# Attention by groups: scores, masks and maxima of the wide tiles one branch at a time, and ScalarE without waits for its own copies and exponentials

## The reference, cut to what matters

```
p_c = masked_softmax(q k_cmp^T * scale)      # 31 compressed blocks
o_s = masked_softmax(q ks^T * scale) vs      # selected blocks; 8 blocks of 64, top 16: all of them, so plain causal
o_w = masked_softmax(q kw^T * scale) vw      # window of 512 of 512 tokens: plain causal too
o   = o_c*gate0 + o_s*gate1 + o_w*gate2
```

## Time and profile before

| | us |
|---|---|
| median of 3 runs | 1486.77 (1486.64 to 1486.95) |
| the profiled execution, time | 1486.48 |
| its span, first to last instruction | 1484.7 |
| PE busy in the span | 1458.0 (98%) |
| DVE busy | 719.7 (48%) |
| ACT busy | 711.5 (48%) |
| POOL busy | 687.1 (46%) |

### The profile page before, as it was taken

The page is one execution under the profiler, slowest core; times in us unless marked ns, Lnnn a source line. Parts: engine busy times, 40 slices in busy tenths (PEclk is TensorE's granted clock), DMA queues, the critical chain, the costliest instruction groups (busy, mean ns, idle before and its releaser), DMA issues.

```text
span 1484.7 us, 23343 instructions
## 1 busy us (share of the span) xinstructions
PE 1458.0 (98%) x7494; PEld 1205.4 (81%) x7494; DVE 719.7 (48%) x1258; ACT 711.5 (48%) x1295; POOL 687.1 (46%) x982
## 2 busy tenths in 40 slices
PE   8999999999999999999999999999999999999998
PEld 6877777888888888888888788888888888888887
DVE  6477774644434300345486767673643444400053
ACT  5245556644444423456464646464654444423262
POOL 5544446665655655364321111203465655655452
PEclk9999999999999999999999999999999999999999
DMA  6311113333222223142410100101233222233221
GB/s 231 105 66 57 57 43 114 128 99 99 86 103 94 99 100 99 57 173 81 143 58 15 44 29 28 40 17 43 100 104 103 90 99 99 95 103 100 85 99 57
DMA packets 38139, 127.80 MB, mean 86 GB/s; under 512 B 6208, under 2 KB 6976, under 8 KB 37824
## 3 DMA queue, kind: packets, MB, share of 16 engines
q1 hardware_dynamic: 32832, 117.46, 23.6%
q10 hardware_dynamic: 5248, 9.55, 1.9%
HBM read 124.90 MB, written 2.10 MB: 86 GB/s over the span
## 4 chain that ended last, share of the span: by engine, by line
PE 41%; issue 33%; POOL 21%; DVE 2%; ACT 2%; DMA 1%; POOLq 0%; SPq 0%; DVEq 0%; ACTq 0%
POOL w_lo L317 21%; PE banks_a L1299 21%; PE banks_a L1309 8%; PE banks_b L1309 7%; PE banks_b L1486 2%; PE banks_a L1505 1%; PE banks_a L1272 1%; DMA x<-in_x 1%; ACT y L384 0%; DVE xn L845 0%; PE banks_b L1489 0%; PE banks_b L1272 0%; ACT w_hi L381 0%; ACT pT L638 0%; DVE amix L1032 0%
## 5 line engine op out<-in xcount | busy, mean ns | idle before, releaser
L317 POOL TENSOR_TENSOR w_lo<-w_raw,w_hi 128x256 fp32r<-128x256 f32 x864 | 657.8, 793 | 737.0 <-ACT w_hi L381 736.7
L381 ACT ACTIVATE w_hi<-w_raw 128x1024 fp32r<-128x1024 f32 x216 | 228.5, 1061 | 271.9 <-PE banks_b L1309 116.2
L1299 PE MATMUL banks_a<-nT_hi,w_hi 128*128 128x512 f32 (+1 forms) x968 | 343.7, 376 | 0.0
L1299 PE MATMUL banks_a<-nT_lo,w_hi 128*128 128x512 f32 (+1 forms) x968 | 342.6, 375 | 0.7 <-DVE nT_lo L851 0.7
L1299 PE MATMUL banks_a<-nT_hi,w_lo 128*128 128x512 f32 (+1 forms) x968 | 341.3, 374 | 0.1
L1299 PEld LDWEIGHTS banks_a<-nT_hi,w_lo 128*128 128x128 f32 x968 | 173.3, 188 | 32.5 <-POOL w_lo L317 0.3
L1299 PEld LDWEIGHTS banks_a<-nT_lo,w_hi 128*128 128x128 f32 x968 | 173.4, 188 | 31.7 <-DVE nT_lo L851 0.9
L1299 PEld LDWEIGHTS banks_a<-nT_hi,w_hi 128*128 128x128 f32 x968 | 173.3, 188 | 31.8 <-ACT nT_hi L414 0.3
L923 DVE SCALAR_TENSOR_TENSOR y<-banks_a,conv,y 128x511 f32<-128x511 f32 x88 | 66.0, 750 | 217.7 <-ACT y L507 217.2
L507 ACT ACTIVATE y<-banks_a,conv 128x512 f32<-128x512 f32 x88 | 68.6, 779 | 206.7 <-PE banks_a L1299 206.6
L1020 DVE TENSOR_REDUCE nm<-banks_b 128x2 f32<-128x256 f32 (+2 forms) x96 | 79.2, 824 | 22.1 <-PE banks_b L1489 10.1
(11 more groups left out here) (275 smaller groups left out, 2364.8 us busy)
## 6 DMA issues: line engine op xcount, KB each, us to landing
w_raw<-in_w SPq DMA_DIRECT2D x216, 512.0 KB, 3.2
g_pre<-in_gains ACTq DMA_DIRECT2D x6, 512.0 KB, 4.9
x<-in_x SPq DMA_DIRECT2D x4, 512.0 KB, 8.5
g_post<-in_gains ACTq DMA_DIRECT2D x4, 512.0 KB, 5.3
out<-x SPq DMA_DIRECT2D x8, 256.0 KB, 2.0
pe_raw<-in_pT ACTq DMA_DIRECT2D x2, 512.0 KB, 5.2
w1k<-in_w ACTq DMA_DIRECT2D x1, 1024.0 KB, 7.0
w1v<-in_w ACTq DMA_DIRECT2D x1, 1024.0 KB, 7.4
```

The source lines that it names most:

```text
L317: pool.tensor_tensor(w_lo[slot][:, cols], w_raw[k % RAW][:, cols], w_hi[slot][:, cols].bitcast(F32), ALU.subtract).then_inc(S["w_lo_done"], 1)
L381: act.activation(w_hi[u % RING][:, :], w_raw[u % RAW][:, :], ACT.Copy).then_inc(S["w_hi_done"], 1)
L1299: m = pe.matmul(bank[:, cols], w[:, k * P:(k + 1) * P], r[:, k, cols], start=(k, pas) == (0, 0), stop=(k, pas) == (KT - 1, 2))
```

## The change

Three edits, all inside the groups.

1. PE: for a wide tile the mask of branch 0 stands right behind its two score matmuls, ahead of branch 1's. Semaphore `gscores_done` rises by 1 with each, as before.
2. DVE: `gmaxima` reduces a wide tile in two instructions, one for each branch, each as soon as its branch is scored. Narrow tiles keep the one reduce. `gnegmax_done` now counts two for each tile, and the own wait of DVE behind it is gone. The helper `maxima`, still used by differential attention, loses an argument.
3. ACT: the exponential of branch c waits for the maximum of branch c only. The exponentials and the copies of `gpT`, `vT`, `pcT` and `Vg` no longer wait for themselves.

```
 # act, gexps
-                        act.wait_ge(S["gnegmax_done"], step(h, k) + 1)
+                        act.wait_ge(S["gnegmax_done"], 2 * step(h, k) + c + 1)
...
-                        signal(act.activation(gp[:, k % 2, c, 0:n], score_columns(k)[:, c, :], ACT.Exp,
-                                              bias=nm[:, qt, c:c + 1],
-                                              accum_out=sums[:, h % 2, qt, c:c + 1]),
-                               "gprobs_done", 2 * step(h, k) + c + 1)
+                        act.activation(gp[:, k % 2, c, 0:n], score_columns(k)[:, c, :], ACT.Exp,
+                                       bias=nm[:, qt, c:c + 1],
+                                       accum_out=sums[:, h % 2, qt, c:c + 1]).then_inc(S["gprobs_done"], 1)
 # act, gp_turned; vT, pcT and Vg in the same way
-                    signal(act.activation(gpT[:, k % 2, 0, 0:n], A[2][:, 0:n], ACT.Copy), "gpTa_done",
-                           step(h, k) + 1)
+                    act.activation(gpT[:, k % 2, 0, 0:n], A[2][:, 0:n], ACT.Copy).then_inc(S["gpTa_done"], 1)
 # dve, gmaxima
-                    maxima(ORDER[k], 2 * (k % 2), "gscores_done", "gnegmax_done", step(h, k), score_columns(k))
+                    qt, both = ORDER[k], score_columns(k)
+                    if qt < 2:
+                        dve.wait_ge(S["gscores_done"], 2 * step(h, k) + 2)
+                        dve.tensor_reduce(nm[:, qt, :], both, AX.X, ALU.max, negate=True)\
+                            .then_inc(S["gnegmax_done"], 2)
+                        return
+                    for c in range(2):
+                        dve.wait_ge(S["gscores_done"], 2 * step(h, k) + c + 1)
+                        dve.tensor_reduce(nm[:, qt, c:c + 1], both[:, c, :], AX.X, ALU.max, negate=True)\
+                            .then_inc(S["gnegmax_done"], 1)
 # pe, gscores, wide tiles
                     for c in range(2):
 
                         for K in (Kh, Kl):
                             pe.matmul(both[:, c, :], Q[h][:, tok(qt)], K[:, c, 0:n], start=K is Kh, stop=False)
-                    for c in range(2):
                         pe.matmul(both[:, c, n - P:n], ident_b[:, :], causal_b[:, :], start=False,
                                   stop=True).then_inc(S["gscores_done"], 1)
```

More of the change, by code:

```diff
@@ L794, in group @@
                 act.wait_ge(S["units_done"], PLAN["group"] + 4 * g + 4)
-                signal(act.activation(vT[:, :], A[2], ACT.Copy), "vT_done", g + 1)
+                act.activation(vT[:, :], A[2], ACT.Copy).then_inc(S["vT_done"], 1)
                 gexps(*seq[0])
                 act.wait_ge(S["cpT_done"], g + 1)
-                signal(act.activation(pcT[:, :, :], A[1].rearrange("p (t n) -> p t n", t=TT), ACT.Copy),
-                       "cpTc_done", g + 1)
+                act.activation(pcT[:, :, :], A[1].rearrange("p (t n) -> p t n", t=TT), ACT.Copy)\
+                    .then_inc(S["cpTc_done"], 1)
                 act.wait_ge(S["vTt_done"], g + 1)
                 v3 = A[0].rearrange("p (t n) -> p t n", t=TT)
-                signal(act.activation(Vg[:, :, :], v3, ACT.Copy), "vg_done", g + 1)
+                act.activation(Vg[:, :, :], v3, ACT.Copy).then_inc(S["vg_done"], 1)
                 gexps(*seq[1])
@@ L1011, in _, with maxima @@
                            4 * half + t + 1)
-            def maxima(qt, b, scores, negmax, step, columns=None):
+            def maxima(qt, b, scores, negmax, step):
                 n = (qt + 1) * P
                 dve.wait_ge(S[scores], 2 * step + 2)
-                if columns is None:
-                    columns = banks_b[:, b:b + 2, 0:n]
-                signal(dve.tensor_reduce(nm[:, qt, :], columns, AX.X, ALU.max, negate=True), negmax, step + 1)
+                signal(dve.tensor_reduce(nm[:, qt, :], banks_b[:, b:b + 2, 0:n], AX.X, ALU.max, negate=True), negmax, step + 1)
             def mix(h, p, qt):
```

## The result

| | before | after |
|---|---|---|
| median of 5 runs each, us | 1486.77 (1485.63 to 1486.95) | 1474.31 (1473.92 to 1475.85) |
| ratio | | 0.9919, 95% interval 0.9904 to 0.9933 |
| profiled execution, time and span | 1486.48, 1484.7 | 1473.99, 1472.2 |

The kernel is faster by 12.5 us, 0.8%.

A forecast was written before the change was run, and what follows sets the result against it. PE was taken as the bound, stalled twice a head by the chain through reduce, exponentials and copy. Saving 2.00 us in each of four groups, 8.0 us, gave 1478.5 profiled, 1478.8 median, range 1475.3 to 1482.8.

The forecast's parts named there:

- What bounds the kernel: Middle heads: a chain through ACT stalls PE 0.55 us at k=1, 0.25 at k=3; without stalls 9.59 us a head.
- The mask's break: PE, wide tiles: a matmul behind the early mask comes 0.08 us later; bounds 0 and 0.28, 32 wide tiles.
- Two reduces: DVE, 512-wide tile: two reduces take 1.41 us against 1.23 for one, 0.18 more, hidden while DVE waits for PE.
- ScalarE's own waits: ACT's exponentials and copies without waiting for themselves: at most 0.12 us for each of three instructions, booked as nothing.
- The first head: First head of a group: DVE's longer reduce makes the k=2 transposes 0.1 us later; PE's idleness becomes a wait there.
- The last head: Last head of a group: k=3 transposes wait 0.61 us by the no-stall rule; DVE's later copy allows 0.35 back.
- The sum: Each group: stalls of 1.65, 0.50 and 0.35 gained, less 0.40 and 0.10, gives 2.00 us; four groups 8.0 us.
- The rival "more": ACT's saved 0.1 us an instruction carries the first head, up to 0.7 more a group: 11 us, 1475.8; chance 12%.

## Why the prediction was half right

- *What bounds the kernel:* right. Two stalls a head, ended by the chain through maxima and exponentials; both are gone and PE is the bound at 9.56 us where I had 9.59 (9.68 in the first of the two middle heads).
- *The mask's break, 0.08 us:* right, 0.08 in the kernel with it alone.
- *Two reduces:* the size was off, 1.29 against my 1.41 (0.06 more than one reduce, not 0.18), since I took the gap from the pair at L1156, and two reduces without a wait between them overlap by 0.09. It changed little: in the middle heads DVE has room. The Trainium skill's rule of large tiles, in "Advanced Engine Details and Errata", section The Read-Write Bubble, speaks against the split; here the split costs DVE 0.06 us a tile.
- *ScalarE's own waits, "I take nothing from it":* the step that failed. I gave 0.12 us for each instruction as the most and booked nothing. Measured it is 0.14 (0.81 to 0.67 for 512 columns), and 0.28 (0.95 to 0.67) once each exponential also waits for its own branch, a cost of the split that I had not seen. It is not slack at the ends of a group: 0.61 us for the third (68.01 and 67.40), and 2.3 us between the first milestone and the end of the span, by the difference of the two kernels.
- *The first head:* I had it 0.1 us worse; it is 0.31 better to the k = 2 transposes (6.68 against 6.99), and 0.21 worse with the own waits kept. The mechanism (DVE decides, the stall moves to k = 2) came true only without the own waits; with them ScalarE still holds k = 1, by 0.85 us.
- *The last head:* I allowed 0.35 of the 0.61 back because DVE's copy seemed to be 0.18 later. All of it came: the k = 3 transposes of the third group start 2.17 behind those of k = 2 (925.99 to 928.16). With the own waits kept 0.33 came, near my number, but by luck: ScalarE held the transposes there and not DVE, with reduces of the same size. It is the own waits once more.
- *The sum:* 2.00 us a group forecast, 2.06 measured in the third group of the kernel with own waits (1.99 to 2.62 over the four), 2.66 to 2.96 with all edits. That 2.06 is so near 2.00 is in part luck, since that kernel's exponentials are dearer than my working had them. The rival "more" named this mechanism at 12% and 11 us; it was the case that came.
- *The whole miss:* I said 1478.5 for the profiled execution and it took 1473.99. Of these 4.5 us the own waits are 2.3, the rest of the groups 0.8 (8.8 with own waits kept, not 8.0, most of it in the first group), and 1.4 lie ahead of the groups and are not the change's. Without that last part the time would have been inside the range.
- *The base:* my range took the median before as it stood, 1486.77. In the two later sets of rounds it is 1.2 us lower, and the difference to the kernel after is 11.5 us instead of 12.5.

## What to carry to other kernels

An instruction that waits for itself cost ScalarE 0.13 to 0.14 us each time here, 0.28 with a second wait behind it, and in a chain that another engine waits for that is time of the kernel: price such waits before anything is split or moved, since here they bring nearly as much alone (1.87 us a group) as the reordering does (2.06), for less text. Two edits on one chain don't add: work out where the next bound lies (here PE's own pace) and cap the sum there. And measure by a period inside the kernel where two versions differ by less than their starts.

## What the runs showed of the hardware that I had not expected

An engine's tiny instruction can wait for POOL. In the kernel after `weights_of_branches` begins like this, DVE first, POOL in the second fence:

```profile
902.49 0.73 DVE L1152 TENSOR_SCALAR st<-sums 128x8 f32<-128x8 f32 x1
```

```profile
901.78 2.78 POOL L317 TENSOR_TENSOR w_lo<-w_raw,w_hi 128x256 fp32r<-128x256 f32 x4 [16.51 <-ACT w_hi L381]
```

In three groups of that kernel it takes 0.72 or 0.73 us, in every other head 0.16 or 0.17. POOL's four pieces are 0.695 long, so the second ends at 903.17 and DVE's instruction at 903.22. With only the exponentials free, POOL works from 902.42 and the same instruction starts at 902.99, shortly before a piece ends, and takes 0.18. So it waits for the end of the piece in progress. The ten traces bear that out: 37 times this instruction starts while POOL works on such a unit, it takes between 0.16 and 0.73 us, and each time that is within 0.02 us of the rest of the piece plus 0.05 (0.16 at the least). With ScalarE's own waits kept it starts 0.01 to 0.03 us ahead of POOL's first piece in three groups, and takes 0.16. No run moved POOL's work alone, and what the two engines share there is left open.

The wait reaches PE. Behind it come DVE's copy and the maxima of k = 2, and these set the exponentials:

```profile
904.44 0.69 DVE L1137 TENSOR_REDUCE nm<-banks_b 128x2 f32<-128x512 f32 x1 [0.21 <-DVE gpT L1148]
...
905.24 0.47 ACT L754 ACTIVATE gp<-banks_b,nm 128x256 f32<-128x256 f32 x1 [1.53 <-PE banks_a L1277]
```

The maxima end at 905.13 and the first exponential starts 0.11 behind that (its bracket names PE, but by the program it needs the transposes of k = 0 only, which end at 902.80), ScalarE's copy ends at 906.74, and the transposes of k = 2 start at 906.85, 2.33 behind those of k = 1. In the first group of the same kernel, where the instruction takes 0.16, they start 2.23 behind. This is the 0.1 us by which the kernel with only the exponentials free is faster in the second head of a group.
